# Hyena half of the first mixer of block two: one stage on even and odd tokens at half of the frequencies, in place of nine stages on whole spectra

## The reference, cut to what matters

```python
def hyena_mix(u, conv_w, conv_b, filt, bias):
    u = dwconv(u, conv_w) + conv_b
    x0, x1, v = jnp.split(u, 3, axis=-1)
    L = u.shape[1]
    g = (v * x1).astype(F32)
    h = hyena_filters(L, *filt)               # a two-layer sine MLP on positions, times a decay
    hf, hb = h[:, :HY_WIDTH], h[:, HY_WIDTH:]
    k2 = jnp.concatenate([hf, jnp.zeros((1, HY_WIDTH), F32), hb[:0:-1]], axis=0)
    n = 2 * L
    y = jnp.fft.irfft(jnp.fft.rfft(g, n=n, axis=1) * jnp.fft.rfft(k2, axis=0)[None], n=n, axis=1)[:, :L]
    y = y + g * bias.astype(F32)
    return y.astype(u.dtype) * x0
```

## Time and profile before

| | us |
|---|---|
| Median of 3 runs (3452.42 to 3454.36) | 3453.66 |
| The profiled execution | 3455.92 |
| Its span, first to last instruction | 3454.1 |
| The nine Hyena stages, from the barrier after mLSTM to the barrier before the split | 207 |
| TensorE busy in the span | 92% |

### The profile page before, as it was taken

The page is one execution under the profiler, slowest core; times in us unless marked ns, Lnnn a source line. Parts: engine busy times, 40 slices in busy tenths (PEclk is TensorE's granted clock), DMA queues, the critical chain, the costliest instruction groups (busy, mean ns, idle before and its releaser), DMA issues. The chain is left out here.

```text
span 3454.1 us, 40249 instructions
## 1 busy us (share of the span) xinstructions
PE 3172.2 (92%) x16286; PEld 2696.9 (78%) x16286; DVE 1877.1 (54%) x2839; ACT 1109.6 (32%) x1639; POOL 100.9 (3%) x78
## 2 busy tenths in 40 slices
PE   7979999999889999999675879999999769999998
PEld 5667888876678888999552359999999756599897
DVE  5744766757457878655464325543554244456464
ACT  4443322334434223433350013221222234333232
POOL 0031000000210000000000010000000000000000
PEclk9988999999989999999886889999999889999999
DMA  3100544521005555221000021121122110033222
GB/s 121 49 25 25 188 160 159 168 70 49 31 14 179 191 178 174 70 98 62 19 1 23 37 87 61 67 69 54 61 71 78 34 45 16 1 122 99 91 95 83
DMA packets 74228, 278.44 MB, mean 81 GB/s; under 512 B 7899, under 2 KB 12507, under 8 KB 72636
## 3 DMA queue, kind: packets, MB, share of 16 engines
q1 hardware_dynamic: 74044, 275.87, 23.7%
HBM read 267.45 MB, written 8.39 MB: 80 GB/s over the span
## 5 line engine op out<-in xcount | busy, mean ns | idle before, releaser
L122 PE MATMUL banks<-normed_hi,weights_hi 128*128 128x384 f32 (+2 forms) x2672 | 886.6, 338 | 6.4 <-DVE normed_lo L1023 6.4
L123 PE MATMUL banks<-normed_lo,weights_hi 128*128 128x384 f32 (+2 forms) x2672 | 884.2, 337 | 0.0
L104 ACT ACTIVATE weights_hi<-weights_raw 128x1024 fp32r<-128x1024 f32 (+3 forms) x365 | 395.7, 1084 | 1273.1 <-PE banks L125 1210.6
L125 PE MATMUL banks<-normed_hi,weights_lo 128*128 128x384 f32 (+2 forms) x2672 | 742.9, 338 | 0.0
L122 PEld LDWEIGHTS banks<-normed_hi,weights_hi 128*128 128x128 f32 x2672 | 503.3, 188 | 34.1 <-DVE normed_lo L1023 6.7
L110 DVE TENSOR_TENSOR weights_lo<-weights_raw,weights_hi 128x1024 fp32r<-128x1024 f32 (+3 forms) x365 | 460.2, 1261 | 128.0 <-ACT weights_hi L104 124.3
L123 PEld LDWEIGHTS banks<-normed_lo,weights_hi 128*128 128x128 f32 x2672 | 505.4, 189 | 27.4
L125 PEld LDWEIGHTS banks<-normed_hi,weights_lo 128*128 128x128 f32 x2672 | 473.0, 189 | 27.5
L123 PE MATMUL banks<-hidden_lo,weights_hi 128*128 128x512 f32 (+1 forms) x880 | 323.0, 367 | 0.0
L122 PE MATMUL banks<-hidden_hi,weights_hi 128*128 128x512 f32 (+1 forms) x880 | 323.0, 367 | 0.0
L125 PE MATMUL banks<-hidden_hi,weights_lo 128*128 128x512 f32 (+1 forms) x880 | 294.7, 367 | 0.0
(11 more groups left out here) (388 smaller groups left out, 4295.7 us busy)
## 6 DMA issues: line engine op xcount, KB each, us to landing
weights_raw<-in_w_up SPq DMA_DIRECT2D x176, 512.0 KB, 3.4
ada_tiles<-in_ada SPq DMA_DIRECT2D x96, 512.0 KB, 3.4
weights_raw<-in_w_down SPq DMA_DIRECT2D x64, 704.0 KB, 4.0
weights_raw<-in_w_in SPq DMA_DIRECT2D x67, 512.0 KB, 3.4
weights_raw<-in_w_out SPq DMA_DIRECT2D x32, 512.0 KB, 3.4
x_kept<-x SPq DMA_DIRECT2D x2, 3072.0 KB, 10.9
x<-x_kept SPq DMA_DIRECT2D x1, 3072.0 KB, 10.3
weights_raw<-in_mla_down SPq DMA_DIRECT2D x6, 512.0 KB, 3.4
```

What stands on the lines that cost most here:

```text
L104: act.activation(self.hi[:, n % 2, 0:w], self.raw[:, n % 2, 0:w], ACT.Copy).then_inc(self.high_ready, 1)
L122: pe.matmul(out, self.hi[:, s, m], xh, start=k == 0, stop=False)
L123: pe.matmul(out, self.hi[:, s, m], xl, start=False, stop=False)
L125: mm = pe.matmul(out, self.lo[:, s, m], xh, start=False, stop=k == kt - 1)
```

## The change

The nine stages become one, with 21 semaphores. It does the latent sequence first and the context after it.

- The tokens of each sequence are split into even and odd ones (strided reads of `hy` and `hid`). At frequency w and at pi - w the cosine and sine sums of even tokens and of odd tokens are the same but for signs, so only half of the frequencies are transformed: `half` makes the sums of the even tokens in one slot of PSUM and those of the odd ones in another, ScalarE copies the odd ones (`odds`) into the unused part of `mixed`, and VectorE forms their sum and difference (`combine`), which are the spectrum at both frequencies. The product of the spectra (`multiply`) then works on both at once, and `back` makes even and odd tokens from their sum and difference at half of the length.
- The sum and the difference of the filter weights are formed once (`fwc`), in place of the sum and difference of the filters. The cleared row becomes a subtraction on one partition (`correct`), with a row of products of its own.
- g's turned tiles are copied by ScalarE (1024 elements a copy), no more by VectorE.
- Tables of context and latent, forward, inverse and decay, have buffers of their own; all eight transfers are issued at the start. The forward and inverse tables have half of the bytes.
- Four PSUM slots of two banks carry all of it. The order of the work on TensorE, ScalarE and VectorE is written out by hand.

The core of the new function; the order of each engine's work is whole:

```diff
+        with stage(nc, "mlp_in", "forward_in", "decay_in", "inverse_in", "gated", "mlp_ready", "mlp_read", "angle_ready",
...
+            @block.sync
+            def _(sp):
+                sp.dma_start(fw[:], dram["filter_w"]).then_inc(mlp_in, 16)
+                sp.dma_start(z[:], dram["positions"]).then_inc(mlp_in, 16)
+                for seg in (1, 0):
+                    sp.dma_start(F[seg][:], dram[f"dft{seg}"]).then_inc(forward_in, 16)
+                for seg in (1, 0):
+                    sp.dma_start(dc[seg][:], dram[f"decay{seg}"]).then_inc(decay_in, 16)
+                for seg in (1, 0):
+                    sp.dma_start(I[seg][:], dram[f"idft{seg}"]).then_inc(inverse_in, 16)
...
+                def turn(slot, tiles):
+                    for b, (seg, p, s) in enumerate(tiles):
+                        t0 = HALVES_OF[seg][0] + 2 * P * s + p
+                        for m in range(4):
+                            mm = pe.transpose(pt[:, slot, b, m * P:(m + 1) * P], hy[:, 8 + m, t0:t0 + 2 * P - 1:2],
+                                              K["ident"])
+                    mm.then_inc(turned, 1)
+
+                def half(slot, p, seg, k, data, ready):
+                    S = 1 + seg
+                    for q in range(2):
+                        for s in range(S):
+                            mm = pe.matmul(pt[:, slot, q], F[seg][:, q, p * S + s, k * P:(k + 1) * P],
+                                           data(q, p * S + s), start=s == 0, stop=s == S - 1)
+                    mm.then_inc(ready, 1)
+
+                def filters(slot, seg, p, s):
+                    t0 = HALVES_OF[seg][0] + 2 * P * s + p
+                    for q in range(2):
+                        mm = pe.matmul(pt[:, slot, q], hid[:, t0:t0 + 2 * P - 1:2], fwc[:, q], start=True, stop=True)
+                    mm.then_inc(filters_ready, 1)
...
+                pe.wait_ge(mlp_in, 32)
+                mlp(0, 0)
+                pe.wait_ge(gated, 1)
+                turn(1, [(1, 0, 0), (1, 0, 1)])
+                turn(2, [(1, 1, 0), (1, 1, 1)])
+                turn(3, [(0, 0, 0), (0, 1, 0)])
+                pe.wait_ge(forward_in, 32)
+                pe.wait_ge(turned_copied, 2)
+                pe.wait_ge(mlp_read, 1)
+                half(0, 0, 1, 0, g(1), even_ready)
+                half(1, 1, 1, 0, g(1), odd_ready)
+                pe.wait_ge(sine_ready, 1)
+                mlp(1, 2)
+                pe.wait_ge(turned_copied, 3)
+                half(3, 0, 1, 1, g(1), even_ready)
+                pe.wait_ge(even_read, 1)
+                half(0, 1, 1, 1, g(1), odd_ready)
+                pe.wait_ge(odd_copied, 1)
+                half(1, 0, 0, 0, g(0), even_ready)
+                pe.wait_ge(mlp_read, 2)
+                half(2, 1, 0, 0, g(0), odd_ready)
+                pe.wait_ge(sine_ready, 2)
+                pe.wait_ge(weights_combined, 2)
+                pe.wait_ge(even_read, 2)
+                filters(3, 1, 0, 0)
+                pe.wait_ge(odd_copied, 2)
+                filters(0, 1, 0, 1)
+                pe.wait_ge(even_read, 3)
+                filters(1, 1, 1, 0)
+                pe.wait_ge(odd_copied, 3)
+                filters(2, 1, 1, 1)
+                pe.wait_ge(shaped, 1)
+                filters(3, 0, 0, 0)
+                pe.wait_ge(shaped, 2)
+                filters(0, 0, 1, 0)
+                pe.wait_ge(shaped, 3)
+                for seg in range(2):
+                    a = HALVES_OF[seg][0]
+                    mm = pe.matmul(pt[0:1, 1, seg], hid[:, a:a + 1], fw[:, 128 + SEQ:128 + 2 * SEQ], start=True, stop=True)
+                mm.then_inc(filters_ready, 1)
+                pe.wait_ge(shaped, 7)
+                half(2, 0, 1, 0, f(1), even_ready)
+                half(3, 1, 1, 0, f(1), odd_ready)
+                half(0, 0, 1, 1, f(1), even_ready)
+                half(1, 1, 1, 1, f(1), odd_ready)
+                pe.wait_ge(even_read, 4)
+                half(2, 0, 0, 0, f(0), even_ready)
+                pe.wait_ge(odd_copied, 4)
+                half(3, 1, 0, 0, f(0), odd_ready)
+                pe.wait_ge(inverse_in, 32)
...
+                pe.wait_ge(spectrum, 2)
+                pe.wait_ge(even_read, 5)
+                pe.wait_ge(odd_copied, 5)
+                for m in range(4):
+                    back(pt[:, m // 2, m % 2], 1, m, cg[0:2]).then_inc(y_ready, 1)
+                pe.wait_ge(spectrum, 3)
+                pe.wait_ge(even_read, 6)
+                for m in range(4):
+                    mm = back(pt[:, 2, m // 2, (m % 2) * CTX:(m % 2 + 1) * CTX], 0, m, cg[2:3])
+                mm.then_inc(y_ready, 1)
...
+                copy(1, gt[1][:, 0:2], 1)
+                copy(2, gt[1][:, 2:4], 2)
+                copy(3, gt[0][:], 3)
+                sine(0, first[:])
+                odds(0, 1)
+                sine(1, hid[:])
+                odds(1, 0)
+                odds(2, 2)
+                odds(3, 3)
+                odds(4, 1)
+                odds(5, 3)
...
+                def combine(n, slot, out):
+                    dve.wait_ge(even_ready, n + 1)
+                    dve.wait_ge(odd_copied, n + 1)
+                    dve.tensor_tensor(out[:, 0], pt[:, slot], odd[n % 2], ALU.add)
+                    dve.tensor_tensor(out[:, 1], pt[:, slot], odd[n % 2], ALU.subtract).then_inc(even_read, 1)
...
+                def correct(seg):
+                    chain.step(dve.tensor_tensor(tmp[:], pt[0:1, 1, seg], dc[seg][0:1, 0], ALU.mult))
+                    x = fl[seg][0:1, :, 0]
+                    return dve.tensor_tensor(x, x, tmp[:].unsqueeze(1).broadcast_to([1, 2, SEQ]), ALU.subtract)
+
+                def multiply(n):
+                    G = cg[n]
+                    dve.wait_ge(even_read, 4 + n)
+                    dve.tensor_tensor(ab[:, 0], G[:], cf[:], ALU.mult)
+                    dve.tensor_tensor(ab[:, 1, :, 0], G[:, :, 1], cf[:, :, 0], ALU.mult)
+                    chain.step(dve.tensor_tensor(ab[:, 1, :, 1], G[:, :, 0], cf[:, :, 1], ALU.mult))
+                    dve.tensor_tensor(ab[:, 0, :, 0], ab[:, 0, :, 0], ab[:, 0, :, 1], ALU.add)
+                    chain.step(dve.tensor_tensor(ab[:, 1, :, 0], ab[:, 1, :, 0], ab[:, 1, :, 1], ALU.subtract))
+                    dve.tensor_tensor(G[:, 0], ab[:, :, 0, 0], ab[:, :, 1, 0], ALU.add)
+                    dve.tensor_tensor(G[:, 1], ab[:, :, 0, 0], ab[:, :, 1, 0], ALU.subtract).then_inc(spectrum, 1)
...
+                dve.tensor_tensor(hy[:, 8:12], hy[:, 8:12], hy[:, 4:8], ALU.mult).then_inc(gated, 1)
+                angle(0, 0)
+                dve.wait_ge(mlp_in, 32)
+                dve.tensor_tensor(fwc[:, 0], fw[:, 128:128 + SEQ], fw[:, 128 + SEQ:], ALU.add).then_inc(weights_combined, 1)
...
+                combine(0, 0, cg[0])
+                angle(1, 2)
+                combine(1, 3, cg[1])
+                combine(2, 1, cg[2])
+                dve.wait_ge(decay_in, 32)
+                for n, (slot, seg, t) in enumerate(((3, 1, 0), (0, 1, 1), (1, 1, 2), (2, 1, 3), (3, 0, 0), (0, 0, 1))):
+                    shape(n, slot, seg, t)
+                dve.wait_ge(filters_ready, 7)
+                dve.wait_ge(shaped, 6)
+                chain.step(correct(1))
+                correct(0).then_inc(shaped, 1)
+                dve.wait_ge(shaped, 7)
+                combine(3, 2, cf)
+                multiply(0)
+                dve.wait_ge(spectrum, 1)
+                combine(4, 0, cf)
+                multiply(1)
+                dve.wait_ge(spectrum, 2)
+                combine(5, 2, cf)
+                multiply(2)
...
```

More of the change, by code:

```diff
@@ L2618, in hyena @@
 def hyena(nc, K, c, hy, dram, mixed):
+    HALVES_OF = [(0, CTX), (CTX, SEQ)]
+    ORDER = [(1, 0), (1, 1), (0, 0)]
     with ExitStack() as ctx:
@@ L2624, in sb @@
             return ctx.enter_context(nc.sbuf_tensor(unique(name), shape, F32))
-        fw = sb("filter_w", [64, 2 * SEQ + 64 + 64])
[L2626 to L2684, removed]
@@ new lines, in over, with held @@
+        def over(name, shape, offset):
+            return nc.alloc_sbuf_tensor_at(unique(name), shape, F32, offset=offset)
+        def held(name, shape):
+            at = (nc.sbuf_base + 31) // 32 * 32
+            return ctx.enter_context(nc.sbuf_tensor(unique(name), shape, F32, align_bytes=32)), at
+        fw = sb("filter_w", [64, 2 * SEQ + 64 + 64])
+        hid = sb("filter_hidden", [64, TOK])
+        fl1, fl_at = held("filters", [P, 2, 4, SEQ])
+        fl = [sb("ctx_filters", [P, 2, 2, SEQ]), fl1]
@@ new lines, in hyena @@
+        gt = [over("ctx_g_tokens", [P, 2, SEQ], fl_at + 4 * SEQ * ROW), over("g_tokens", [P, 4, SEQ], fl_at)]
+        dc1, dc_at = held("filter_decay", [P, 4, SEQ])
+        dc = [sb("ctx_filter_decay", [P, 2, SEQ]), dc1]
+        cf = over("f_combined", [P, 2, 2, SEQ], dc_at)
+        F = [sb("ctx_dft", [P, 2, 2, P]), sb("dft", [P, 2, 4, 2 * P])]
+        I = [sb("ctx_idft", [P, 2, 1, 2, P]), sb("idft", [P, 2, 2, 2, 2 * P])]
```

(24 more changed lines are left out.)

175 lines of the change are left out of this document (78 added, 97 removed).

## The result

Median 3354.33 us of four executions (3350.11 to 3363.05) against 3453.04 of the kernel before; ratio 0.9718, interval 0.9697 to 0.9739. That is 98.7 us less; 3368 was forecast, with 3350 to 3388 as the range. The profiled execution is the slowest of the four, 3363.05, and must be compared with its own: before 3455.92, so 92.9 us less. 3.9 of these lie before the Hyena part begins (its first instruction starts at 1817.32, had 1821.18), in code that is the same; 88.8 are the stage itself, 117.9 against 206.7.

A forecast was written before the change was run, and what follows sets the result against it. No engine was taken as full: Hyena's stages stand in a row, each waiting for its slowest part. The new path summed to 121.0 us against 206.7, a gain of 85.7, giving 3370.2 profiled and 3368 median, range 3350 to 3388.

The forecast's parts named there:

- 6, `correct`: Two corrections of the cleared row after the filter products, priced as for all 128 partitions: 4.0 us.
- 8, VectorE's chain: Copy, then combine and multiply twice on VectorE before the inverse, with `multiply` at 9.3 us: 24.6 us.
- 9, inverse and last four `leave`: Latent inverse 16.0 us including a new clock climb, context inverse 3.6, then drain and the context's `leave`.
- Step 2: Even and odd `half` for the first latent block, 16 records with a 4.5 us clock climb: 9.1 us.
- Step 5: Seven groups of two filter products, taken at half clock: 23.9 us and 0.2 of drain.
- the rival's 3356: Filter products keep the full clock, taking 12.0 us in place of 23.9: total 3356, chance 28%.
- the idle stretch is as long as the one that dropped: TensorE stands 2.7 us before the filter products, a reason given for taking them at half clock.
- The transfers were hidden: The eight early table transfers were to cost nothing, hidden by the transposes, with no transfer wait after the first.
- Strided reads: Reads of every second element, priced as adjacent ones; the rival of double price was +13 us, 3381, chance 7%.
- The rival of a low clock nearly everywhere: TensorE's clock stays low nearly everywhere because work comes in pieces with gaps: +35 us, 3403, chance 8%.
- Slower than before: Strided weight loads for transposes and filter products take long enough to lose the gain: 3462 at 1.8 us more each, chance 1%.
- TensorE starts at 0.50 after each barrier: Clock reading of the old kernel's rows, with a climb taken as 4.5 us of work.

The follow-up runs named there:

- again: The changed kernel run once more with no edit, profiled in one of its faster executions: 3353.64 to 3367.93 us, ratio 0.9727.
- fill_gap: Changed kernel with one pair of products made twice to fill TensorE's idle gap before the filter products: 3354.98 us, ratio 0.9715.
- late_inverse: Changed kernel with the two inverse tables issued only after the second spectrum is done: 3360.53 us, ratio 0.9733.
- own_tables: The kernel before the change, with only its full-size tables given own buffers and issued in its first stage: 3437.30 us, ratio 0.9953.
- rows128: Changed kernel with 24 records of filter products zero-padded from 64 to 128 rows: 3353.07 us, ratio 0.9711.
- early_row: Changed kernel with the cleared row's products made first and their subtractions placed between the decay multiplications: 3356.87 us, ratio 0.9719.
- warm_inverse: Changed kernel with seven products that nobody reads made while TensorE waits before the inverse: 3350.81 us.
- twice: Changed kernel with every half-frequency sum made twice, as much work as whole spectra: 3378.41 us, ratio 0.9785.
- wide128: Changed kernel with both the longer idle gap of wide_gap and the zero-padding of rows128: 3356.98 us.
- wide_gap: Changed kernel with the first filter products waiting for the third combination, not the second, widening TensorE's idle gap: 3368.16 us.
- second_fill: Changed kernel with filled gap before the filter products, early row, unread products before the inverse, and two more before the filter's spectra: 3348.69 us, ratio 0.9698.

## Why the prediction was right, and where not

The path held, step by step, in the profiled execution. That execution happens to be of the kind that was forecast (filter products at half clock), which two of eight were; with again's, the stage would have missed the forecast by 13.6 us and not by 3.1. Lengths from the timeline above, forecast first:

| Step | forecast | measured |
|---|---|---|
| 1, MLP product and transposes | 12.4 | 12.0 |
| 2, two `half` | 9.1 | 7.0 |
| 3, copy, `combine`, `angle` | 9.7 | 9.5 |
| 4, sine, copy, `combine` | 4.4 | 4.4 |
| 5, filter products | 24.1 | 22.9 |
| 6, `correct` | 4.0 | 4.0 |
| 7, two `half` | 9.2 | 9.8 |
| 8, VectorE's chain | 24.6 | 24.8 |
| 9, inverse and last four `leave` | 23.5 | 23.5 |
| Stage | 121.0 | 117.9 |

- Step 2 was mis-sized by 2.1 us: I let the climb begin with the first `half`. The window from 1822 to 1848.4 has 0.89 on average, which is 5.8 us at half clock and the rest at full, so it rose at about 1827.8, during the transposes (1824.76 to 1829.16). This was not so early in every profile: in again all 24 transposes ran at 0.50 (5.4 us) and the clock rose at 1833.7, 0.4 us after the first `half` began. In none of the twelve profiles of the new stage did it rise later than 0.6 us after that. The Trainium skill ("TensorE: Matmul & The Clock Gate", "Part 4: PE-mode transpose") says that transposes do not count as busy for the clock; here it rose while they ran, 2.8 us of MLP products before them (in fill_gap too), so the traces speak against it.
- Step 5 is where the forecast of the median failed. I put 55% on half clock and 28% on full clock (3356). For one execution the mechanism was priced well: 12 us between the groups was forecast, the stages are 10.6 apart. But it is not one or the other for the kernel. It differs from execution to execution, two of eight slow, and a median then is the commoner case: 3354.3, the rival's 3356. That the median lies inside the range is owed to the range, which took in the rival. The step that failed is "the idle stretch is as long as the one that dropped": it was 1.9 us, not 2.7 (TensorE's sums of g took 0.5 longer, VectorE's chain 0.3 less), and the earlier trace rows had one stretch of each kind at about 2.5, which spoke for both outcomes within one kernel rather than for one of them. What else than the length decides is open.
- The transfers were hidden, as said; late_inverse and own_tables give their price, 6 us in the new order and 15 in the old. Strided reads cost nothing that shows: at half clock throughout, 24 transposes took 5.4 us in again, where 5.5 was forecast from adjacent ones (they took 4.4 in the timeline above because the clock rose while they ran), and the last `leave` 0.42, as forecast for adjacent ones. `multiply`'s 2048 elements took 2.29, as extrapolated. `correct` cost as if all partitions took part, the upper bound.
- The rival of a low clock nearly everywhere fell: the stretches of full rows all climbed. Slower than before was never near.

One reading of the rows was wrong: "TensorE starts at 0.50 after each barrier". In the kernel before, the stage that turns the latent g starts at 1898.41, behind a barrier, at 1.00:

```profile
1898.00:1902.50 4.50, 2.32 (x16) 1.70 (x16) 2.58 (x4) 0.00 (x0) 0.00 (x0) 1.00 0.00 0
```

The 64-row products of the next stage began at 1.00 too, at 1902.54, and lost it within 0.2 us, so not all three stretches began low. The sum is not hurt by it, as the new stage did start at 0.50.

Between the profile before and again's the stage lost 99.4 us: TensorE is busy 66.2 less (144.7 to 78.5) and stands 33.2 less (62.0 to 28.9). Of the 99 us of the median, shown by edits: about 15 for early tables alone in the old order, 24.4 for the half spectra in the new one. The inverse's halved columns (17 by count) and the eight barriers with what waited at them were not tried by themselves; since parts overlap, the rest is not split further.

## What to carry to other kernels

Follow the path engine by engine with durations from neighbouring rows, and price every gap in which TensorE stands twice: once for its length, once for the clock afterwards. A gap that the clock may or may not survive turns into executions of two kinds, so one profile does not stand for the median; look at the spread and at each execution's mean clock first. Where TensorE waits anyway, a few products that nobody reads can be cheaper than standing, provided they end before the wait does.

## What the runs showed of the hardware that was not expected

- After 1.9 us of standing the granted clock fell in one profile (1.4 us after work had resumed) and stayed at 1.00 in five (again, rows128, late_inverse, early_row, warm_inverse); after 4.1 us it fell in both profiles, 1.1 us after work had resumed. Behind the filter products it fell sooner in six profiles, 0.8 to 1.2 us after the last product, and in three others (fill_gap, twice, wide128) after 2.4 to 4.1.
- 64-row products at 0.50 stayed there for 22.0 us, zero-padded to 128 rows they rose after 3.4; begun at 1.00, 64-row ones stayed there for 12.4 in again, and lost it after 2.1 in own_tables. The Trainium skill ("TensorE: Matmul & The Clock Gate", "Why this matters for your kernels") advises against long idle gaps between bursts of products. wide_gap's 4.1 us bear it out; here gaps of 1.9 and 2.2 us could cost a climb too, and filling the second saved 2.8 us (second_fill).
- Padding with zeros cost nothing on TensorE: 24 records at 592 ns against 589.
